# One tap of a short convolution moved from VectorE to ScalarE, between the halves of a weight tile

## The reference

```python
D_FF, CONV_WIDTH_2 = 2816, 3
def causal_dwconv(x, w, b):     # one filter of three taps for each channel
    y = lax.conv_general_dilated(x, w[:, None, :].astype(x.dtype), window_strides=(1,),
        padding=[(CONV_WIDTH_2 - 1, 0)], dimension_numbers=('NWC', 'WIO', 'NWC'),
        feature_group_count=C)
    return y + b

hn = rms_norm_2(h, ffn_pre_norm)
u = causal_dwconv(hn @ w_up, conv_w, conv_b)
gate, up = jnp.split(u, 2, axis=-1)
y = (jax.nn.gelu(gate, approximate=True) * up) @ w_down
return h + rms_norm_2(y, ffn_post_norm)
```

## Time and profile before

| | |
|---|---|
| median of three runs | 1430.54 us |
| the profiled execution | 1429.88 us, with a span of 1428.10 us |
| PE matmuls busy in the span | 1326.5 us (93%) |
| DVE busy | 919.7 us (64%) |
| ACT busy | 586.8 us (41%) |
| mean granted clock of TensorE | 0.914 of full speed |
| up2, about | 1206 to 1354 us from the span's start |

### The profile page before, as it was taken

The page is one execution under the profiler, slowest core; times in us unless marked ns, Lnnn a source line. Parts: engine busy times, 40 slices in busy tenths (PEclk is TensorE's granted clock), DMA queues, the critical chain, the costliest instruction groups (busy, mean ns, idle before and its releaser), DMA issues.

```text
span 1428.1 us, 25070 instructions
## 1 busy us (share of the span) xinstructions
PE 1326.5 (93%) x9306; PEld 1218.2 (85%) x9306; DVE 919.7 (64%) x1654; ACT 586.8 (41%) x1003; POOL 61.7 (4%) x52
## 2 busy tenths in 40 slices
PE   5899989899999999989999999999799976999996
PEld 5888879799999999668899999989656666899996
DVE  5876347576665577645657666577853346999955
ACT  4644344454444522424344444533533323444441
POOL 0554100000000000000000000000000000000000
PEclk9999999999999999559999999999955568999998
DMA  6434344245555544102325555534410003355462
GB/s 243 145 120 147 118 155 170 79 158 178 187 191 180 181 174 150 58 1 95 142 89 177 176 183 191 209 136 165 155 53 1 1 4 116 118 176 172 162 213 73
DMA packets 29589, 194.19 MB, mean 136 GB/s; under 512 B 3152, under 2 KB 6352, under 8 KB 6352
## 3 DMA queue, kind: packets, MB, share of 16 engines
q1 hardware_dynamic: 29520, 193.22, 39.1%
HBM read 192.16 MB, written 1.05 MB: 135 GB/s over the span
## 4 chain that ended last, share of the span: by engine, by line
PE 72%; DVE 18%; issue 5%; ACT 2%; DVEq 1%; DMA 1%; ACTq 0%; SPq 0%
PE acc L405 17%; PE acc L407 16%; PE acc L406 16%; PE acc L421 8%; PE sc L588 6%; DVE wlo L978 4%; PE acc L609 3%; PE tp L600 2%; DVE wlo L975 2%; PE sc L591 1%; ACT whi L715 1%; DVE E L1173 1%; DVE nw L1027 1%; DVE nw L1026 1%; PE st L561 1%
## 5 line engine op out<-in xcount | busy, mean ns | idle before, releaser
L405 PE MATMUL acc<-Hhi,whi 128*128 128x256 f32 x1504 | 435.7, 290 | 39.3 <-DVE wlo L978 24.5
L406 PE MATMUL acc<-Hlo,whi 128*128 128x256 f32 x1504 | 427.8, 284 | 0.0
L407 PE MATMUL acc<-Hhi,wlo 128*128 128x256 f32 x1504 | 427.7, 284 | 0.0
L715 ACT ACTIVATE whi<-raw 128x1024 fp32r<-128x1024 f32 x164 | 173.4, 1057 | 476.5 <-PE acc L407 445.8
L405 PEld LDWEIGHTS acc<-Hhi,whi 128*128 128x128 f32 x1504 | 290.9, 193 | 47.1 <-issue 23.7
L406 PEld LDWEIGHTS acc<-Hlo,whi 128*128 128x128 f32 x1504 | 291.0, 194 | 2.1 <-issue 1.9
L407 PEld LDWEIGHTS acc<-Hhi,wlo 128*128 128x128 f32 x1504 | 290.8, 193 | 0.0
L975 DVE TENSOR_TENSOR wlo<-raw,whi 128x1024 fp32r<-128x1024 f32 x164 | 200.8, 1224 | 136.0 <-ACT whi L715 134.6
L405 PE MATMUL acc<-FH,whi 128*128 128x256 f32 x848 | 243.4, 287 | 20.9 <-DVE wlo L978 5.2
L407 PE MATMUL acc<-FH,wlo 128*128 128x256 f32 x848 | 242.9, 286 | 0.0
L978 DVE TENSOR_TENSOR wlo<-raw,whi 128x1024 fp32r<-128x1024 f32 x164 | 202.0, 1232 | 0.0
(11 more groups left out here) (213 smaller groups left out, 1702.5 us busy)
## 6 DMA issues: line engine op xcount, KB each, us to landing
raw<-weights SPq DMA_DIRECT2D x180, 1024.0 KB, 4.9
cst<-consts SPq DMA_DIRECT2D x1, 1126.0 KB, 12.3
X<-x_in SPq DMA_DIRECT2D x1, 1024.0 KB, 6.1
MEM<-mem_in SPq DMA_DIRECT2D x1, 1024.0 KB, 14.4
out<-X SPq DMA_DIRECT2D x4, 256.0 KB, 2.2
PT<-positions SPq DMA_DIRECT2D x1, 128.0 KB, 14.2
cst<-consts SPq DMA_DIRECT2D x1, 32.0 KB, 1.9
```

What stands on the lines that cost most here:

```text
L405: pe.matmul(dst, w, x, start=first, stop=False)
L406: pe.matmul(dst, w, xl, start=False, stop=False)
L407: return pe.matmul(dst, wl, x, start=False, stop=last)
L715: act.activation(whi[j][:, 0:HALF, :], raw[j][:, 0:HALF, :], ACT.Copy).then_inc(hi_out, 1)
```

## The change

ScalarE gets the first of the three taps, a scaled copy into E, for gate and for up. It stands between the two halves of `split`. On VectorE the two multiplies of the first tap are gone. The first half of its low part (L975) moves ahead of the convolution and the second (L978) stays behind it, for both tiles of a turn. VectorE waits on a new semaphore `first_tap` ahead of the multiply-adds. In the first turn both halves made after the gate tile stay ahead of the norm; there ScalarE makes the tap by itself behind its two halves.

```diff
@@ ScalarE
-            def split(load, j, done=None):
+            def split(load, j, done=None, between=None):
                 act.activation(whi[j][:, 0:HALF, :], raw[j][:, 0:HALF, :], ACT.Copy).then_inc(hi_out, 1)
+                if between:
+                    between()
                 act.activation(whi[j][:, HALF:KC, :], raw[j][:, HALF:KC, :], ACT.Copy).then_inc(hi_out, 1)
...
+                def tap(i, j, src):
+                    def first():
+                        acc_out(name, 2 * i + j)
+                        for c in range(2):
+                            w = cst[:, bass.ds(12 * i + (C0["cw2"][0] + 6 * j + 3 * c), 1)]
+                            ins = act.activation(E[:, j, c, :], src[:, c, 0:S], ACT.Copy, scale=w)
+                        ins.then_inc(first_tap, 1)
+                    return first
...
-                        ahead(name, i, 2, 0)
+                        ahead(name, i, 2, 0, between=tap(i, 0, TG) if conv and start else None)
+                        if conv and not start:
+                            tap(i, 0, TG)()
...
-                        ahead(name, i, 2, 1)
+                        ahead(name, i, 2, 1, between=tap(i, 1, TU) if conv else None)
@@ VectorE
-            def lower(j, after):
+            def lower(j, after, between=None):
                 dve.wait_ge(hi_out, after + (-1))
                 dve.tensor_tensor(out=wlo[j][:, 0:HALF, :], in0=raw[j][:, 0:HALF, :], in1=f(whi[j][:, 0:HALF, :]),
                                   op=ALU.subtract)
+                if between:
+                    between()
                 dve.wait_ge(hi_out, after)
...
+                elif between:
+                    out_acc(ins())
+                    ahead(name, i, 2, j, between=more)
...
-                for tap in range(3):
+                for tap in (1, 2):
                     for k in range(2):
                         w = col("cw2", 3 * (c + k) + tap)
-                        s_ = src[:, k, tap:tap + S]
-                        if tap == 0:
-                            ins = dve.tensor_scalar(dst[:, k, :], s_, w, None, op0=ALU.mult)
-                        else:
+                        if tap == 2:
                             ch.wait(before[k])
-                            ins = dve.scalar_tensor_tensor(out=dst[:, k, :], in0=s_, scalar=w, in1=dst[:, k, :],
-                                                           op0=ALU.mult, op1=ALU.add)
+                        ins = dve.scalar_tensor_tensor(out=dst[:, k, :], in0=src[:, k, tap:tap + S], scalar=w, in1=dst[:, k, :],
+                                                       op0=ALU.mult, op1=ALU.add)
...
                         def gate_conv():
-                            dve.wait_ge(acc_free, 2 * i + (G0[name] + 3))
+                            dve.wait_ge(first_tap, 2 * i + 1)
                             short_conv(E[:, 0, :, :], TG, 4 * i).then_inc(s_given, 1)
 
                         def up_conv():
-                            dve.wait_ge(acc_free, 2 * i + (G0[name] + 4))
+                            dve.wait_ge(first_tap, 2 * i + 2)
                             ch.link(short_conv(up, TU, 4 * i + 2))
```

More of the change, by code:

```diff
@@ L219, in build @@
         stat_ready, rt_ready, spread_ready, st_used = (sem(n) for n in ("stat_ready", "rt_ready", "spread_ready", "st_used"))
-        gain_loaded = sem("gain_loaded")
+        gain_loaded, first_tap = sem("gain_loaded"), sem("first_tap")
         tokens_ready, hid_turned, hid_copied = sem("tokens_ready"), sem("hid_turned"), sem("hid_copied")
@@ L715, in split, with ahead @@
                 act.activation(whi[j][:, 0:HALF, :], raw[j][:, 0:HALF, :], ACT.Copy).then_inc(hi_out, 1)
+                if between:
+                    between()
                 act.activation(whi[j][:, HALF:KC, :], raw[j][:, HALF:KC, :], ACT.Copy).then_inc(hi_out, 1)
-            def ahead(name, i, per, k, last=False):
+            def ahead(name, i, per, k, last=False, between=None):
                 t = T0[name] + k
                 if not last and (isinstance(i, int) and WHOLE0 <= per * i + t + 2 < WHOLE1) is False:
-                    split(16 * (per // 2) * i + 16 * (t // 2 + 2), k % 2, per * i + (t + 1))
+                    split(16 * (per // 2) * i + 16 * (t // 2 + 2), k % 2, per * i + (t + 1), between)
             def acc_out(name, g):
@@ L979, in lower, with ahead @@
                                   op=ALU.subtract).then_inc(lo_dve, 1)
-            def ahead(name, i, per, k, last=False):
+            def ahead(name, i, per, k, last=False, between=None):
                 t = T0[name] + k + 2
                 if not last and (isinstance(i, int) and WHOLE0 <= per * i + t < WHOLE1) is False:
-                    lower(k % 2, 2 * per * i + 2 * (t + 1 - (WHOLE1 - WHOLE0 if t >= WHOLE1 else 0)))
+                    lower(k % 2, 2 * per * i + 2 * (t + 1 - (WHOLE1 - WHOLE0 if t >= WHOLE1 else 0)), between)
             def tile(name, i, per, k):
@@ L1091, in first_turn, with evacuate @@
                 return ((0, 1), (1, eng_loop)) if norm_name and eng_loop > 1 else ((0, eng_loop),)
-            def evacuate(name, i, j, ins, norm_name, more=None):
+            def evacuate(name, i, j, ins, norm_name, more=None, between=False):
                 tile(name, i, 2, j)
@@ L1181, in conv_ffn @@
                 for start, stop in first_turn(11, norm_name):
-                    with ch.loop(stop, 5 + 6 + (0 if start else NORM_LINKS), start) as i:
+                    with ch.loop(stop, 3 + 4 + (0 if start else NORM_LINKS), start) as i:
                         def gate_conv():
-                            dve.wait_ge(acc_free, 2 * i + (G0[name] + 3))
+                            dve.wait_ge(first_tap, 2 * i + 1)
                             short_conv(E[:, 0, :, :], TG, 4 * i).then_inc(s_given, 1)
                         def up_conv():
-                            dve.wait_ge(acc_free, 2 * i + (G0[name] + 4))
+                            dve.wait_ge(first_tap, 2 * i + 2)
                             ch.link(short_conv(up, TU, 4 * i + 2))
-                        evacuate(name, i, 0, times_r(TG[:, :, 2:2 + S], 0), norm_name, gate_conv)
+                        evacuate(name, i, 0, times_r(TG[:, :, 2:2 + S], 0), norm_name, gate_conv, between=True)
                         if start:
@@ L1195, in conv_ffn @@
                             dve.wait_ge(s_h, i + h.at(name, 0))
-                        evacuate(name, i, 1, times_r(TU[:, :, 2:2 + S], 1), norm_name, up_conv)
+                        evacuate(name, i, 1, times_r(TU[:, :, 2:2 + S], 1), norm_name, up_conv, between=True)
                         dve.wait_ge(s_taken, 2 * i + taken.at(name, 1))
```

## The result

The changed kernel took 1425.48 us (median of seven runs, 1422.75 to 1426.23), the kernel before 1430.60 (seven runs, 1429.55 to 1432.23). By the medians that is 5.1 us faster. The ratio, which is taken of the means, is 0.9958 with a 95% interval of 0.9946 to 0.9970, that is 6.0 us faster (4.3 to 7.7). The forecast was a median of 1423.9, 6.6 us faster: the median is 1.6 us above it and inside its range. The profiled execution has a span of 1422.1 us, against 1428.1.

What follows compares the result with a forecast made beforehand. VectorE was taken to bound the up stage, TensorE after the change: -7.80 us over 20 tiles, +1.28 first turn, a 0.10 restart gone, -6.6 in all, median 1423.9 us; range 1422.6 to 1424.9, wider range to 1427.4.

Steps and rivals of the forecast that it cites:

- The bound and the turn: Up stage: VectorE sets turns of 12.31 us; after the change TensorE sets 11.52, read from stage gu1.
- The hand-over: From ScalarE's taps to VectorE's multiply-adds: unknown price between 0.03 and 0.18 us, taken as 0.18.
- The slack: Time before TensorE wants the next load: 0.30 us in the gate half, only 0.09 in the up half.
- the restart of 0.10 in the rivals: Late up half (chance 0.20) and slower hand-over (0.05): each missed load pays 0.10 us for TensorE's restart besides its lateness.
- The rule of the Trainium skill: VectorE's next instruction starts only when the pipe is empty: up half misses by 0.09, 1.9 us in ten turns, 1425.8.
- The first turn: First turn of the up stage: nothing covers the gate taps, so it costs +1.28 us.
- The clock: Rival: TensorE's clock falls after the first turn's longer pause, 17 slow matmuls, 1.6 us, 1425.5; chance 0.07.

Runs made afterwards that it cites:

- 10: The changed kernel without the first tap on either engine, so the result lacks it: 1424.38 us, ratio 0.9948.
- 1: The changed kernel with ScalarE's tap kept but VectorE in the old order, convolution first and both halves behind it: 1443.36 us, ratio 1.0093.
- 7: The changed kernel plus one more scaled copy on ScalarE ahead of the up tile's taps in turns 1 to 10: 1426.58 us, ratio 0.9966.
- 8: The changed kernel plus one more scaled copy on ScalarE ahead of the gate tile's taps: 1424.85 us, ratio 0.9951.
- 9: The changed kernel plus the extra up-half copy, with VectorE's wait for the last multiply-add moved behind the second half: 1425.65 us, ratio 0.9960.
- experiment 6: The changed kernel without an edit, run for a third profile: 1424.89 us, one run.
- 2: The changed kernel's order on VectorE, but VectorE makes all three taps itself: 1429.63 us, ratio 0.9995.
- 12: The new order with VectorE making all three taps, and the second tile's weights split first in the first turn: 1427.29 us, ratio 0.9974.
- experiment 5: The changed kernel without an edit, run for a second profile: 1426.47 us, one run.

## Why the prediction was right

*The bound and the turn.* Right, to the hundredth: VectorE set 12.31, TensorE sets 11.52, as read in gu1. That ScalarE's tap costs nothing in these turns is shown by 10, and that this hangs on VectorE's first half as a cover by 1.

*The hand-over,* taken as 0.18 between 0.03 and 0.18: 0.17 in the loop (7), 0.03 in the first turn, where the addresses are constants (ScalarE's taps end at 1225.21, VectorE starts at 1225.24).

*The slack.* The 0.09 in the up half and the 0.30 in the gate half are borne out by 7 and 8: the same copy costs 0.12 a turn in the one and nothing in the other, and 9 gives it back. Mis-sized was the restart of 0.10 in the rivals, which counted the late load twice. The rule of the Trainium skill (VectorE: DVE Perf Modes, The DRAIN you can't avoid) that I set against the forecast (1425.8) did not come true, though the measured median lies close to its number: in the up half the multiply-adds start 1287.40 - 1286.26 = 1.14 behind a first half of 1.23, the second half starts 1289.19 - 1287.40 = 1.79 behind them, as in the sum, and the turns stayed at 11.52. The same section of the Trainium skill goes on that a next instruction which nothing holds starts earlier; I had left that out, and the trace agrees with it.

*The first turn.* I gave +1.28; the trace has (1231.68 - 1223.58) - (1229.71 - 1222.78) = +1.17, since the static form of the linked four is 0.09 shorter than the loop's. What I had not seen: ScalarE's table load for the gelu was hidden under the norm before and now follows the first tap, at 1225.23. It is hidden again, by VectorE's multiply-adds, with 0.44 us to spare, so it cost nothing; that was luck, as the prediction did not have it. The Trainium skill (ScalarE: Activation LUTs, What ACT_TABLE_LOAD costs) gives 1283 ns for the load and about 1380 ns more for a drain; the trace shows the 1.28 us (its end is 1226.51), but the gelu starts at 1226.95, released by VectorE, where 1.38 us more would make it 1227.89. So here the measurement is shorter than the total of the Trainium skill.

*The clock.* I gave a fall of TensorE's clock in the first turn 0.07 and 1.6 us. The size was right (1.5 us: 120.5 against 119.0). The chance was not: it was there in 2 of 3 profiles of the changed kernel. That the median, 1425.48, equals this rival's number is no proof of it. The profile that was taken first shows the full 6.8 us inside the stage and behind it; with a fall of 1.5 us in two of three executions the mean gain would be 5.8, an estimate, and the means differ by 6.0. That is consistent, but the scatter upstream (3.2 us) is larger than the fall, and experiment 6 had the fall and took 1424.89, less than the median. So the fall is a likely part of the 1.6 us by which the median lies above the forecast; what each timed run owes to it and what to the scatter is not shown, since they have no trace.

*The order without the tap* was worth less than I thought in 2 and 12 (no gain, and 3.6 us with weights first). In 2, most of what the later turns gave went into the first turn (+1.29) and the second (+1.12). A VectorE that is the bound can't make up for the 1.30 us in which it waits for TensorE; by the rows that wait comes from the slow matmuls behind the pause and hardly from the pause itself.

## What to carry to other kernels

Moving work from the engine that sets the pace to an idle one pays only if the receiving engine's time lies under something that the first engine does meanwhile: the tap without the order cost 13 us, the order without the tap brought nothing as it stood, both together 6. Take the floor of a stage from a stage of the same kernel with the same tiles in which the other engine never waits, and look at start times, not at busy matmuls. Look at the turn that is written out by itself: it has none of the loop's cover, and here putting the next weights before everything else gave 2.4 us more than the change, by the distance in the stage.

## What the runs showed of the hardware

TensorE's clock can fall to 1.2 GHz after a pause of 2.7 us in one execution and not in the next, of the same kernel. By gaps between the starts of matmuls at that place of the stage, 5 of the 8 profiles with 2.86 us or more had it, and none of the 6 with 2.04 or less. The slow stretch does not begin right behind the pause: matmuls ran at 2.4 GHz for 0.8 us (experiment 1) to 1.6 us (experiment 5) first, then 15 ran at 1.2 GHz, for 1.4 us more than they need. The Trainium skill (TensorE: Matmul & The Clock Gate, What's actually happening) says of the start of a kernel that the number of slow matmuls varies from run to run of the same kernel. Here, behind a pause, it was 0 in one profile of the changed kernel and 15 in two.

The traces show more than chance in it. From the rise of the clock at the head of up2 to the first matmul behind the pause are 22.32 to 23.06 us in the five profiles with the fall, and 22.13 to 22.27 in the three without; and in all five the clock falls 23.89 us behind that rise. By these eight, what differs from one execution to the next is where the kernel's work lies against the clock's own moments, here by some hundredths of a us. No run moved the pause alone to test this. So one profile with granted clock 1.00 does not show that a pause is harmless.

A weight load that came 0.13 us late made the turn 0.12 longer (7): counted from the moment at which the load is wanted, the lateness was the whole price, and a first matmul of 0.38 in place of 0.28 the sign of it. Counted by the start of the first matmul the price is some 0.10 more than one sees, since the matmul behind it comes 0.22 later and not 0.12. In the kernel before, the first matmul came 0.31 - 0.12 = 0.19 late in one half turn and 0.54 - 0.12 = 0.42 in the other:

```profile
1292.11 0.28 PE L407 MATMUL acc<-Hhi,wlo 128*128 128x256 f32 x1
1292.65 0.38 PE L405 MATMUL acc<-Hhi,whi 128*128 128x256 f32 x1 [0.26 <-DVE wlo L978]
```

With 0.09 more behind each of the two that makes the 0.79 us which a turn gained.
